# Attention values with the value columns stationary, two heads on the two output halves, and outputs, z and half the first gate kept feature-major

## What is computed

```
# first block: gated delta rule (dn) beside windowed attention with sinks (sw)
proj = rms_norm(x, norm_w) @ w_in            # split into dn_q.., dn_z, .., sw_q, sw_k, sw_v, sw_z
sw = windowed_gqa_with_sinks(...)            # 8 query heads of 64, 2 key/value heads
sw = sw * silu(sw_z)
dn = rms_norm(gated_deltanet_bidir(...)) * silu(dn_z)
x  = x + concat([dn, sw]) @ w_out
# second block: chunked attention beside a gated convolution
att   = softmax(q @ k.T * scale + bias) @ v  # 8 heads of 64
y_att = (att * silu(z_att)) @ w_att_out
m     = sigmoid(g_att) * y_att + sigmoid(g_conv) * y_conv
out   = rmsnorm(x + m @ w_out_2)
```

## Time and profile before

| | |
|---|---|
| median of 3 runs | 4115.74 us (4115.09 to 4117.45) |
| the profiled execution's own time | 4121.41 us |
| its span, first to last instruction | 4119.6 us |
| PE busy | 3520.2 us (85%), 19766 matmuls |
| DVE, ACT, POOL busy | 1389.0, 1164.6, 360.7 us |
[...]

### The profile page before, as it was taken

The page is one execution under the profiler, slowest core; times in us unless marked ns, Lnnn a source line. Parts: engine busy times, 40 slices in busy tenths (PEclk is TensorE's granted clock), DMA queues, the critical chain, the costliest instruction groups (busy, mean ns, idle before and its releaser), DMA issues. The chain is left out here.

```text
span 4119.6 us, 53171 instructions
## 1 busy us (share of the span) xinstructions
PE 3520.2 (85%) x19766; PEld 3004.9 (73%) x19766; DVE 1389.0 (34%) x2326; ACT 1164.6 (28%) x1942; POOL 360.7 (9%) x356
## 2 busy tenths in 40 slices
PE   6997998549999987198896988899899979958979
PEld 5776788548888887166685877788778858846767
DVE  5552001545444454844544000121100014433333
ACT  4221111424344433167103111100012126631032
POOL 0000000012222221500210000000000001110000
PEclk8998999979999998589897999999999979978989
DMA  3122122831121111330543111100021132034453
GB/s 108 66 72 86 46 74 76 255 105 67 66 83 62 62 67 51 108 117 33 184 165 128 61 69 64 51 31 31 32 80 61 71 128 70 13 114 147 154 167 126
DMA packets 183098, 365.92 MB, mean 89 GB/s; under 512 B 30064, under 2 KB 105712, under 8 KB 169456
## 3 DMA queue, kind: packets, MB, share of 16 engines
q1 hardware_dynamic: 167472, 328.77, 23.1%
q10 hardware_dynamic: 15552, 36.18, 2.5%
HBM read 231.07 MB, written 133.82 MB: 89 GB/s over the span
## 5 line engine op out<-in xcount | busy, mean ns | idle before, releaser
L924 DVE COPY_PREDICATED ds_z<-ds_masks,ds_ps 128x512 f32<-128x512 int32 x192 | 140.5, 732 | 310.2 <-PE ds_ps L1003 310.2
L1003 PE MATMUL ds_ps<-ds_ut,ds_neg_m 128*128 128x128 f32 x1536 | 220.0, 293 | 0.0
L106 PE MATMUL ps_pp<-h_hi,ps_whi 128*128 128x512 f32 x512 | 200.0, 391 | 15.3 <-DVE ps_wlo L1808 15.3
L1003 PEld LDWEIGHTS ds_ps<-ds_ut,ds_neg_m 128*128 128x128 f32 x1536 | 205.8, 209 | 7.2 <-issue 7.2
L106 PE MATMUL gc_pp<-h_hi,gc_whi 128*128 128x512 f32 x512 | 199.9, 390 | 10.3 <-DVE gc_wlo L1901 10.3
L108 PE MATMUL gc_pp<-h_hi,gc_wlo 128*128 128x512 f32 x512 | 199.7, 390 | 0.0
L107 PE MATMUL ps_pp<-h_lo,ps_whi 128*128 128x512 f32 x512 | 199.7, 390 | 0.0
L107 PE MATMUL gc_pp<-h_lo,gc_whi 128*128 128x512 f32 x512 | 199.7, 390 | 0.0
L108 PE MATMUL ps_pp<-h_hi,ps_wlo 128*128 128x512 f32 x512 | 199.6, 390 | 0.0
L106 PE MATMUL pc_pp<-h_hi,pc_whi 128*128 128x512 f32 x384 | 151.9, 396 | 20.0 <-DVE pc_wlo L327 19.8
L1003 PE MATMUL ds_ps<-ds_z,ds_ut 128*128 128x128 f32 x1280 | 164.8, 280 | 0.0
(11 more groups left out here) (308 smaller groups left out, 8173.6 us busy)
## 6 DMA issues: line engine op xcount, KB each, us to landing
ds_pk<-scratch_pack SPq DMA_DIRECT2D x32, 1280.0 KB, 7.3
scratch_sig_fm<-ps_ob SPq DMA_DIRECT2D x16, 1024.0 KB, 3.9
mb_sg<-scratch_sig_fm SPq DMA_DIRECT2D x16, 1024.0 KB, 8.4
scratch_qkv_fm<-pc_acc SPq DMA_DIRECT2D x12, 1024.0 KB, 4.9
dp_fm<-scratch_qkv_fm SPq DMA_DIRECT2D x16, 768.0 KB, 6.5
scratch_pack<-dp_out SPq DMA_DIRECT2D x16, 768.0 KB, 3.3
n_x<-in_x SPq DMA_DIRECT2D x16, 512.0 KB, 4.5
scratch_gate_rows<-pg_ob SPq DMA_DIRECT2D x32, 256.0 KB, 2.0
```

Source lines behind the costliest of these rows:

```text
L106: nc.tensor.matmul(out, ah, bh, start=(first and i == 0), stop=False)
L924: nc.vector.copy_predicated(z[d][:, n], masks[:, d * len(LEVELS) + n + 1, :].unsqueeze(1).to_broadcast([P, 4, P]), heads(ps[d][:, 0, :])). ...
L1003: mm = nc.tensor.matmul(out_of(h), lhs_of(h), rhs_of(h), start=True, stop=True)
```

## The change

`values` handles both heads of a pair in one loop: 64 value columns of a key tile are stationary and the 128 columns of the transposed probabilities move; head 0 writes output partitions 0 to 63 and head 1 partitions 64 to 127 of one PSUM tile. The output is so feature-major, and the denominators must be laid out the same way: DVE takes the reciprocal of 4 numbers a row broadcast to 128x256 (`denominators(.., half)`, now twice a tile), PE turns that with two transposes (`spread`), ACT copies the result to SBUF (`copy_spread`), and DVE multiplies (`finish`). The order of this work between the heads is new on DVE, ACT and PE. The attention outputs are stored feature-major (`sw_fm`, `att_fm`, pieces of 512 bytes). The gate of sw and z are made feature-major too: a new stage `ph` of `project_features` in place of the second group of `pg`, and `pz` becomes `project_features`. `mix_output` turns only the dn half, POOL multiplies the sw half by its gate, and ACT waits for the split of tile t+1 before it requests tile t+3, now with five loads. `merge_branches` has no transposes: ACT and DVE split what POOL wrote, and SP waits for DVE's split before it loads a slot again. The host reorders `w_out` and the gate's weights for sw to match.

```diff
-            def values(now, m, g):
+            def values(now, m):
                 t, u, s, lo, n, b0 = now
                 M = PAIRS * t + m
                 half = m // 2
-                pe.wait_ge(pt_copied[g], M + 1 + START)
-                if m % 2 == 0 and g == 0:
+                for g in G:
+                    pe.wait_ge(pt_copied[g], M + 1 + START)
+                if m % 2 == 0:
                     wait(pe, half_done[half], t)
-                v0 = value_at(m, g)
                 for a in range(n):
-                    mm = nc.tensor.matmul(o_ps[half][:, 2 * (m % 2) + g, 0:HD], prt[m % 2][g][:, a * P:(a + 1) * P],
-                                          v[s][:, a, v0:v0 + HD], start=(a == 0), stop=(a == n - 1))
-                mm.then_inc(weighed[g], 1)
+                    for g in G:
+                        v0 = value_at(m, g)
+                        mm = nc.tensor.matmul(o_ps[half][HD * g:HD * g + HD, m % 2, :], v[s][:, a, v0:v0 + HD],
+                                              prt[m % 2][g][:, a * P:(a + 1) * P], start=(a == 0), stop=(a == n - 1))
+                        if a == n - 1:
+                            mm.then_inc(weighed[g], 1)
...
+            def spread(now, half):
+                t, u, s, lo, n, b0 = now
+                pe.wait_ge(den_inv[half], t + 1 + START)
+                for r in range(2):
+                    mm = nc.tensor.transpose(o_ps[half][:, 2 + r, :], rden[half][:, r, :], ident[:])
+                mm.then_inc(spread_done[half], 1)
...
                 if t2:
-                    values(t2, m2, 0)
-                    values(t2, m2, 1)
+                    values(t2, m2)
                 if t1:
                     turn(t1, m1, 1)
+                if t2 and m2 % 2:
+                    spread(t2, m2 // 2)
...
-            def denominators(now):
+            def denominators(now, half):
...
+                wait(dve, spread_done[half], t)
+                nc.vector.reciprocal(rden[half][:].rearrange("p r (g d) -> p (r g) d", g=2),
+                                     den[s][:, 0, at].unsqueeze(2).to_broadcast([P, 4, HD])).then_inc(den_inv[half], 1)
 
...
-                    dve.wait_ge(weighed[g], PAIRS * t + 2 * half + 2 + START)
+                dve.wait_ge(rd_copied[half], t + 1 + START)
...
+                nc.vector.tensor_tensor(ob[s][:, 2 * half:2 * half + 2, :], o_ps[half][:, 0:2, :], rd[half][:],
+                                        ALU.mult).then_inc(half_done[half], 1)
...
-                        if h == 0 and sinks and before:
-                            sink_minus_max(before)
-                        if h == 3 and before:
-                            denominators(before)
+                        if h == 0 and before:
                             finish(before, 0)
-                        if h == 5 and before:
+                        if h == 2 and before:
+                            denominators(before, 1)
+                        if h == 3 and sinks:
+                            sink_minus_max(now, 0)
+                        if h == 5:
+                            denominators(now, 0)
+                        if h == 6 and before:
                             finish(before, 1)
+                        if h == 7 and sinks:
+                            sink_minus_max(now, 1)
                         if after and 4 <= h < 4 + nk_tiles:
...
+            def copy_spread(now, half):
+                t, u, s, lo, n, b0 = now
+                act.wait_ge(spread_done[half], t + 1 + START)
+                nc.scalar.copy(rd[half][:], o_ps[half][:, 2:4, :]).then_inc(rd_copied[half], 1)
...
-                act.dma_start(out[t].rearrange("p (h d) -> p h d", h=8), ob[s][:]).then_inc(stored[s], 16)
+                act.dma_start(out[:, :, bass.ds(t * P, P)].rearrange("m p t -> p m t"), ob[s][:]).then_inc(
+                    stored[s], 16)
...
                 for m in range(PAIRS):
                     which, mm = lagged(before, now, m, 1)
+                    if m == 0 and before:
+                        copy_spread(before, 0)
+                    if m == 2 and before:
+                        copy_spread(before, 1)
...
-                        sink_exponent(before)
+                        if m == 0 and g == 0 and sinks and before:
+                            sink_exponent(before, 1)
+                        if m == 2 and g == 0 and sinks:
+                            sink_exponent(now, 0)
...
             i, s, u = of_pair(j, t)
             for d in range(2):
                 eng.dma_start(of[s][:, d, :], delta_o[d, i]).then_inc(m["rows_in"][s], 16)
-            eng.dma_start(mix[s][:, W:DM], sw_o[i]).then_inc(m["rows_in"][s], 16)
             eng.dma_start(gate[s][:], gate_rows[i]).then_inc(m["rows_in"][s], 16)
+            at = bass.ds(i * P, P)
+            eng.dma_start(sw[s][:], sw_fm[:, :, at].rearrange("m p t -> p m t")).then_inc(m["rows_in"][s], 16)
+            eng.dma_start(gsw[s][:], gate_fm[:, :, at].rearrange("m p t -> p m t")).then_inc(m["rows_in"][s], 16)
...
+                    nc.gpsimd.tensor_tensor(sw[s][:], sw[s][:], gsw[s][:], ALU.mult).then_inc(m["sw_gated"][s], 1)
...
+                nc.vector.tensor_tensor(mlo[s][:, 0:4, :], pt[s][:].rearrange("p (k t) -> p k t", k=4),
+                                        mhi[s][:, 0:4, :].bitcast(F32), ALU.subtract)
+                nc.vector.tensor_tensor(mlo[s][:, 4:8, :], sw[s][:], mhi[s][:, 4:8, :].bitcast(F32),
                                         ALU.subtract).then_inc(m["lo_ready"][s], 1)
...
+                nc.scalar.copy(mhi[s][:, 0:4, :], pt[s][:].rearrange("p (k t) -> p k t", k=4))
+                act.wait_ge(m["sw_gated"][s], u + 1 + START)
+                nc.scalar.copy(mhi[s][:, 4:8, :], sw[s][:]).then_inc(m["hi_ready"][s], 1)
 
             def step(j, t, follow):
+                i, s, u = of_pair(j, t)
                 if follow > 0:
                     split_hi(j, t + 1)
                 if follow > 2:
+                    act.wait_ge(m["lo_ready"][1 - s], u + s + 1 + START)
+                    act.wait_ge(const_in, 32 + START)
                     load_rows(act, j, t + 3)
                 if follow > 1:
...
-                for k in range(KT):
+                for k in range(4):
                     mm = nc.tensor.transpose(pt[s][:, k * P:(k + 1) * P], mix[s][:, k * P:(k + 1) * P], ident[:])
...
             def _(sp):
-                sp.dma_start(ident[:], consts[:, C_ID * P:(C_ID + 1) * P]).then_inc(const_in, 16)
                 with sp.Fori(0, H) as j:
                     for s in S:
-                        sp.wait_ge(turned[s], j + START)
-                        sp.wait_ge(const_in, 16 + START)
-                        sp.dma_start(att[s][:], att_o[2 * j + s]).then_inc(rows_in[s], 16)
-                        sp.dma_start(zr[s][:], z_rows[2 * j + s]).then_inc(rows_in[s], 16)
+                        at = bass.ds(j * (2 * P) + s * P, P)
+                        sp.wait_ge(a_lo[s], j + START)
+                        sp.dma_start(att[s][:], att_fm[:, :, at].rearrange("m p t -> p m t")).then_inc(rows_in[s], 16)
+                        sp.dma_start(zr[s][:], z_fm[:, :, at].rearrange("m p t -> p m t")).then_inc(rows_in[s], 16)
...
-            @block.tensor
-            def _(pe):
-                pe.wait_ge(const_in, 16 + START)
-                with pe.Fori(0, H) as j:
-                    for s in S:
-                        pe.wait_ge(gated[s], j + 1 + START)
-                        pe.wait_ge(a_lo[s], j + START)
-                        for k in range(K4):
-                            mm = nc.tensor.transpose(pt[s][:, k * P:(k + 1) * P], att[s][:, k * P:(k + 1) * P], ident[:])
-                        mm.then_inc(turned[s], 1)
...
-                            act.wait_ge(turned[s], j + 1 + START)
-                            nc.scalar.copy(ahi[:, :, bass.ds(j * (2 * P) + s * P, P)],
-                                           pt[s][:].rearrange("p (k t) -> p k t", k=K4)).then_inc(a_hi[s], 1)
+                            act.wait_ge(gated[s], j + 1 + START)
+                            nc.scalar.copy(ahi[:, :, bass.ds(j * (2 * P) + s * P, P)], att[s][:]).then_inc(a_hi[s], 1)
...
-                            nc.vector.tensor_tensor(alo[:, :, at], pt[s][:].rearrange("p (k t) -> p k t", k=K4),
-                                                    ahi[:, :, at].bitcast(F32), ALU.subtract).then_inc(a_lo[s], 1)
+                            nc.vector.tensor_tensor(alo[:, :, at], att[s][:], ahi[:, :, at].bitcast(F32), ALU.subtract).then_inc(a_lo[s], 1)
...
-            project_rows(nc, "pg1", d["w_gate1"], 2, 512, hi, lo, gate_rows, ACT.Silu)
+            project_rows(nc, "pg1", d["w_gate1"], 1, 512, hi, lo, gate_rows, ACT.Silu)
+            project_features(nc, "ph", d["w_gate_fm1"], 4, hi, lo, gate_fm, ACT.Silu)
...
-            project_rows(nc, "pz", d["w_z2"], 1, 512, hi, lo, z_rows, ACT.Silu)
```

(1 more changed line is left out.)

## The result

The changed kernel takes 4153.81 us (median of 4 runs, 4150.81 to 4156.85) beside 4116.59 for the kernel before (median of 4 runs, 4115.09 to 4128.9); the ratio is 1.0078, 95% interval 1.0058 to 1.0098. Its profiled execution has a span of 4150.5 us at a mean granted TensorE clock of 0.919 of full speed, against 4119.6 at 0.919: +30.9. The forecast was 4114, no change, with 4100 to 4128 as its own range; the sign of the result was given 0.43, and rival 2 (a reciprocal of over 1.5 us) 0.17. The time lies inside the wide range of 4090 to 4188, as that of a rival.

A forecast was written before the change was run, and what follows sets the result against it. It took PE to bound attention and `mo`, loads the start of `mb`. `wa` +16, `ca` -26, dense stages +13.6, `mo` -8.5 and `mb` +3 made -2 us on 4115.74: 4114, own range 4100 to 4128, wide range 4090 to 4188.

The forecast's parts named there:

- rival 2: Attention stages `wa` and `ca`: DVE's 256-number reciprocal takes over 1.5 us and makes the kernel slower; chance 0.17.
- Column halves: Value matmuls in attention: both heads' halves run together, 1.12 us a pair of `ca` instead of 2.18.
- Rival 3: Value matmuls in attention: the column halves don't run together, kernel +74, 4190 us; chance 0.22.
- The 0.34 us for a change of array shape: PE in attention: switching to half-array form and back costs 0.34 us, twice a pair with the new values, 0.68.
- I take 1.27: DVE in attention: a reciprocal of 256 numbers takes 1.27 us, by a straight line through 1 and 10 elements.
- the prediction's own formula for `wa`: Stage `wa`: DVE's loop worked out step by step, tile 12.75 us against 11.8, together +16 us.
- the other insertions stay at or under PE's time: Stage `ca`: DVE's `finish` (0.42 us) and key copy (some 0.5) don't delay PE; tile 16.7 us, stage -26.
- rival 4: Clock in `ca`: its half-speed start may end a tile sooner or later, 8 to 10 us each way; no separate chance.
- +0.5 a pair of tiles: Start of `mb`: splits replace transposes in the slot's loop, +0.5 us with handovers; stage about +3, between -1 and +6.
- the steady gain: Stage `mo`: four transposes fewer on PE, -0.44 us a tile, x 15 = -6.6 us.
- The start: Start of `mo`: one chain (gate of 512, four transposes at half clock twice) gets 2 us shorter.
- Dense stages: Gaps and feature tiles: first block +11.2 us, second +2.4, together +13.6.

The follow-up runs named there:

- experiment 3: Changed kernel with `values` going over head 0's key tiles first, then head 1's, so the column halves no longer alternate: 4174.2 us.
- experiment 9: Changed kernel, reciprocal taken of 256 plain numbers for a tile's first half, of 64 numbers then laid out by a copy for the second: 4134.03 us.
- experiment 1: Changed kernel with DVE taking the reciprocal of 4 numbers only and PE laying it out by four small matmuls: 4118.45 us, ratio 0.9993 to the kernel before.
- experiment 2: Changed kernel with the reciprocal of 4 numbers a row, laid out over 256 columns by a DVE copy: 4118.5 us.
- experiment 5: Changed kernel with the second half's 256-wide reciprocal behind the second `neg` of pair 1 and PE's turn of it behind `scores(2)`: 4130.97 us.
- experiment 6: Changed kernel with reciprocal of 4 numbers plus copy, and all DVE's other work only behind a pair's second `neg`, none behind the last: 4094.6 us.
- experiment 8: Kernel before with four slots instead of two for att and z at the start of `mb`: 4104.87 us, ratio 0.9957.
- experiment 10: Changed kernel without POOL's multiply of sw by its gate in `mo`, so its output leaves that gate out: 4154.82 us.

## Why the prediction was wrong

- **Column halves** (forecast): right. Pitch 0.055 us, undisturbed pair 2.69 and 3.91 us for 2.66 and 3.98. Experiment 3 shows that it hangs on their alternating. Rival 3 (0.22) is refuted: both halves use all rows, and they run together. The pitch is 0.109 us with 64 moving columns and 0.112 with 128, and with 64 stationary columns one half by itself keeps the same 0.109 us (experiment 3). What sets it, no run here shows. The 0.34 us for a change of array shape, taken twice a pair, is a remainder of the author's sums, and no run shows it as a thing of its own. Taken the same way, with values at 0.055 us a record, the remainder in the kernel after is 3.91-(1.09+1.09+1.10) = 0.63 us a pair in `ca` and 2.69-(0.65+0.65+0.66) = 0.73 in `wa`, for the 0.68 of the forecast.
- **The reciprocal** (step "I take 1.27"): mis-sized, and this is the term that turned the result. 1.753 us measured. The slope from 1 and 10 numbers, 4.3 ns, was carried to 256; it is 6.3 ns from 64 to 256 (experiment 9). With 1.753 the prediction's own formula for `wa`, 28 insertions, gives 16+28x0.48 = +29.4; measured +27.8. That alone puts the sum at -2+40x0.48 = +17: slower by more than 0.2%. Of the 33 us between the forecast's -2 and the +31 of the profiles these 19 are the largest part; `mb` (7.5), `mo` (4.5) and `dp` (2.8) follow. Rival 2's mechanism is the one that happened, and experiments 1, 2 and 5 show it by size and by place.
- **`ca`** (step "the other insertions stay at or under PE's time"): wrong. 17.2 us was due with the measured reciprocal, 17.6 came. The last key copy was not worked out against the next tile's first scores, which wait 0.70 us for it. Removing it, with the rest of the order, gave 16.09 in experiment 6, near PE's own time.
- **`ca`, the clock** (rival 4): it moved the other way and hid part of this. The third tile took 20.33 us at a granted clock of 0.50 in the profile before, 13.46 at 1.00 after, and 11.64 at 0.98 with the old attention code in experiment 8. About 8.7 us of the -20.1 belong to when the clock rose, which is luck, and only some 11.6 to the change (268.0 against 279.6). It isn't tied to the kernel: the same experiment 8 lost 6.4 us on the second tile of `wa` (17.69 at 0.58 for 11.33 at 0.96).
- **`mb`** (step "+0.5 a pair of tiles"): mis-sized. The round grew by 1.2 us in the first half. Its parts: ACT's and DVE's splits in the loop as forecast, and DVE's split at 1.26 us instead of 0.69 where it lies beside POOL's multiply, now that it reads `mb_att` in SBUF (the kernel before read `mb_pt` in PSUM; its splits stay at 0.67 to 0.69 us beside POOL too, there and in experiment 8). Nearly half of the loss is one round, the one at half way: 10.8 us between the multiplies at 3723.71 and 3734.53, where the kernel before has 6.0 (3696.95 to 3702.97). The prediction named it and gave it too little. The slot's split stands behind DVE's split of the branch, and the load now waits for it:

```profile
3728.96 1.75 DVE L2096 TENSOR_TENSOR mb_alo<-mb_att,mb_ahi 128x512 f32 x1
...
3730.87 0.37 SPq L2062 DMA_DIRECT2D mb_att<-scratch_att_fm  x1
...
3734.53 1.26 POOL L2073 TENSOR_TENSOR mb_att<-mb_att,mb_zr 128x512 f32<-128x512 f32 x1 [4.37 <-DMA mb_zr<-scratch_z_fm]
```

Together +10.5, above the stated top of +6.
- **`mo`**: the steady gain was right (11.63 for 12.04 a tile, -0.41 for -0.44). The start was wrong: from ACT's first operation to the first product it is not 2 us shorter but 1 longer (28.8 for 27.7). POOL's third operation beside DVE's multiplies accounts for 1.8 us (experiment 10). ACT's late `root`, which the prediction held to be covered, isn't at the second tile: PE stands still 1.25 us longer there, more than the saved transposes gave.
- **Dense stages**: right, +11.6 and +2.4 for +11.2 and +2.4.
- **`dp`**: not in the sum at all. 132.7 and 132.9 us in two kernels with the old layout, 135.4 to 139.3 in the eleven of the new one, its code untouched. Busy time by window of `dp`'s first 16 us and of the rest, before (first two lines) and after:

```profile
703.60:719.60 16.00, 9.95 (x52) 8.79 (x53) 8.48 (x14) 6.74 (x9) 0.00 (x0) 0.71 0.52 167
719.60:836.30 116.70, 70.42 (x526) 63.77 (x524) 59.97 (x98) 52.21 (x71) 0.00 (x0) 0.94 0.78 251
```

```profile
715.40:731.40 16.00, 11.36 (x48) 9.87 (x48) 8.47 (x14) 6.03 (x9) 0.00 (x0) 0.52 0.49 153
731.40:850.70 119.30, 70.39 (x528) 63.97 (x528) 59.97 (x98) 52.63 (x72) 0.00 (x0) 0.94 0.76 247
```

The granted clock of the first 16 us is 0.52 instead of 0.71, but little of the time is lost there. Counted from the stage's first matmul, ACT's copy of `dp_tok_p` for the third of the 16 tiles starts at 19.2 us for 18.6, for the fifth at 38.0 for 35.7. In experiment 1 the third comes at 18.1, sooner than before, and the stage still takes 139.0. So the low clock at the start doesn't explain it by itself; the cause stays open. Moving `ph` behind `pr` did not bring 132.7 back.

The common root of the two large errors: a price extrapolated by a factor of 25 in size was used as a point, where the time that DVE has to spare at each insertion decided whether it cost anything, and that time was worked out for some insertions and not for the key copies.

## What to carry to other kernels

A small operation put into an in-order queue costs by its place. Between the two operations that free the next step's input it delays that step by all that the engine has no time to spare for (here the step grew by 1.49 us in `wa` and 0.98 in `ca` for a reciprocal of 1.75, PE's turn of it included); behind the second one it is free up to the time in which the engine waits for that step anyway: there the same 1.75 us left a tile of `wa` at 12.85 us for 13.47 (experiment 5), and with 0.47 us and the rest of DVE's work there no row of PE in the steady tiles waits for DVE (experiment 6). Take a reciprocal of the few numbers there are and lay out the result afterwards; 0.47 us did what 1.75 did. When a bound engine gets faster, walk through every copy and load that used to be in time; here the last key copy made each tile of `ca` wait 0.70 us, where the tile had won 1.2 in all.

## What the runs showed of the hardware

- Two matmuls of 64 stationary columns each on the two column halves of TensorE, both over all 128 rows, ran at once where they alternated: 0.055 us a record (kernel after, 20 in 1.31 us), against 0.109 for one half by itself (experiment 3) and for 128 stationary columns.
- DVE's float32 reciprocal took 0.17 us for 4 numbers a row (experiment 2), 0.55 for 64 (experiment 9) and 1.75 for 256 (256 plain numbers in experiment 9 or 4 repeated 64 times in the kernel after alike); a copy of 4 numbers over 256 took 0.29 (experiment 2).
- DVE's two-input operations on 512 columns from SBUF took 0.69 us alone and mostly 1.1 to 1.75 beside a POOL operation of 512 columns (kernel after: 1.14 to 1.75 in `mb`, 1.26, 1.41 and 1.63 in `mo`). In some overlaps it was POOL's that took longer: beside DVE's splits of 2048 columns up to 3.3 us for 1.26 (kernel after, two multiplies in 6.45 us from 3723.71) and 2.39 (kernel before, 3699.10). With one input in PSUM, DVE's split of 512 columns stayed at 0.67 to 0.69 us beside POOL (kernel before, experiment 8).
